# Pairing the heads of the gated linear attention, and loading constants later, in a hybrid encoder kernel

## The reference

```
def gla_chunk(S, inp):                       # one chunk of 64 frames, state S [64 x 128] per head
    q, k, v, la = inp
    b = cumsum(la, axis=2)                   # log decay
    decay = exp(where(causal, b[t] - b[s], -inf))            # per key channel
    scores = einsum('bhtd,bhsd,bhtsd->bhts', q, k, decay)
    o = einsum('bhts,bhsv->bhtv', scores, v) + einsum('bhtd,bhdv->bhtv', q * exp(b), S)
    S_new = exp(b_end)[..., None] * S + einsum('bhsd,bhsv->bhdv', k * exp(b_end - b), v)
    return S_new, o
```

## Time and profile before

| | |
|---|---|
| runs | 3391.13, 3376.59, 3386.97 us, median 3386.97 |
| profiled execution | 3374.3 us, span 3372.3 us, mean granted TensorE clock 0.977 |
| PE busy | 3237.7 us, 96% of the span |
| PE weight loads busy | 2759.2 us, 82% |
| DVE, ACT, POOL busy | 56%, 49%, 28% |
| DMA | 356.61 MB, mean 106 GB/s |

### The profile page before, as it was taken

The page is one execution under the profiler, slowest core; times in us unless marked ns, Lnnn a source line. Parts: engine busy times, 40 slices in busy tenths (PEclk is TensorE's granted clock), DMA queues, the critical chain, the costliest instruction groups (busy, mean ns, idle before and its releaser), DMA issues. The chain is left out here.

```text
span 3372.3 us, 48730 instructions
## 1 busy us (share of the span) xinstructions
PE 3237.7 (96%) x18362; PEld 2759.2 (82%) x18362; DVE 1882.9 (56%) x3387; ACT 1663.6 (49%) x3129; POOL 929.4 (28%) x570
## 2 busy tenths in 40 slices
PE   6999999999977999999999999999999999999999
PEld 5777777787767888888988888898878887899998
DVE  2463544544436555554676766677778776323333
ACT  3443343523327555554566665567666665233332
POOL 0231321411311233333323232322222223333332
PEclk9999999999886999999999999999999999999999
DMA  4553443533336223332523233242222223422221
GB/s 138 154 173 105 143 143 105 176 99 105 99 102 175 79 82 103 94 107 80 174 76 95 85 99 105 88 150 68 84 76 88 93 71 101 135 67 84 76 87 66
DMA packets 272378, 356.61 MB, mean 106 GB/s; under 512 B 59713, under 2 KB 188754, under 8 KB 271122
## 3 DMA queue, kind: packets, MB, share of 16 engines
q1 hardware_dynamic: 272146, 353.50, 33.4%
HBM read 295.91 MB, written 57.54 MB: 105 GB/s over the span
## 5 line engine op out<-in xcount | busy, mean ns | idle before, releaser
L1825 POOL TENSOR_TENSOR st_ul<-st_ur,st_uh 128x1024 fp32r<-128x1024 f32 x144 | 343.3, 2406 | 845.1 <-ACT st_uh L1634 845.1
L1832 POOL TENSOR_TENSOR st_dl<-st_dr,st_dh 128x1024 fp32r<-128x1024 f32 x144 | 342.0, 2397 | 775.5 <-ACT st_dh L1644 775.5
L1799 DVE TENSOR_TENSOR st_ya<-st_ya,st_dp 128x512 f32<-128x512 f32 x544 | 369.1, 682 | 132.1 <-PE st_dp L1556 129.7
L1727 DVE TENSOR_TENSOR_SCAN st_g<-st_z,st_g,st_a 128x127 f32<-128x127 f32 (+3 forms) x336 | 371.3, 1105 | 19.9 <-DVE st_g L1716 0.5
L1786 DVE TENSOR_TENSOR st_tl<-st_dp,st_th 128x512 fp32r<-128x512 f32 (+3 forms) x166 | 96.6, 582 | 464.6 <-ACT st_dp L1682 464.5
L1601 ACT ACTIVATE st_a<-st_z 128x128 f32<-128x128 f32 (+3 forms) x336 | 177.1, 527 | 356.0 <-PE st_z L1415 214.8
L491 PE MATMUL fr_pj<-fr_wl,fr_xh 128*128 128x512 f32 x816 | 335.6, 411 | 0.0
L1556 PE MATMUL st_dp<-st_dh,st_tl 128*128 128x512 f32 x1020 | 335.2, 400 | 0.0
L1556 PE MATMUL st_dp<-st_dl,st_th 128*128 128x512 f32 x1020 | 334.9, 400 | 0.0
L1556 PE MATMUL st_dp<-st_dh,st_th 128*128 128x512 f32 x1020 | 334.3, 400 | 0.0
L1438 PEld LDWEIGHTS st_po<-st_v,st_wt 128*128 128x128 f32 x2256 | 310.7, 199 | 28.6 <-DMA st_v<-out_new_v 3.2
(11 more groups left out here) (169 smaller groups left out, 6063.9 us busy)
## 6 DMA issues: line engine op xcount, KB each, us to landing
st_ur<-in_w_up SPq DMA_DIRECT2D x60, 1024.0 KB, 5.3
st_dr<-in_w_down SPq DMA_DIRECT2D x60, 1024.0 KB, 4.9
fr_wr<-in_w_in SPq DMA_DIRECT2D x96, 512.0 KB, 3.9
k_t<-fr_stT SPq DMA_DIRECT2D x21, 512.0 KB, 4.4
fr_xb<-in_x SPq DMA_DIRECT2D x17, 512.0 KB, 5.5
q_t<-fr_stT SPq DMA_DIRECT2D x17, 512.0 KB, 4.6
st_ya<-in_x SPq DMA_DIRECT2D x17, 512.0 KB, 5.7
st_qh<-q_t SPq DMA_DIRECT2D x64, 128.0 KB, 6.2
```

Of the source, the lines that this page charges most:

```text
L1727: ins = dve.tensor_tensor_scan(g[:, u % 2, n - 2::-1], z[:, u % 2, n - 1:0:-1], a[:, u % 2, n - 2::-1], g[:, u % 2, n - 1:n], ALU.add, ALU ...
L1799: dve.tensor_tensor(part, part, dp[:, k % BANKS], ALU.add).then_inc(s_fd, 1)
L1825: pool.tensor_tensor(ul[:, c], ur[:, c], raw(uh[:, c]), ALU.subtract).then_inc(s_ul, 1)
L1832: pool.tensor_tensor(dl[:, k], dr[:, k], raw(dh[:, k]), ALU.subtract).then_inc(s_dl, 1)
```

## The change

In the linear attention the two heads of a pair are issued alternately. `sc0` and `sc1` (and `sc2`, `sc3`) are taken together: both banks are waited for, then the 7 multiplications of the head in partitions 0 to 63 and those of the head in 64 to 127 alternate, each head to its own bank. The output has two banks, `po0` for even and `po1` for odd heads; for each pair `sm` x `v` of both heads is followed by four multiplications of 64 rows and 64 columns, one for each head and chunk, each writing only the 64 rows of its chunk. The zero halves of `qb` and the semaphore `s_oe` go; ACT copies two half banks where it copied one bank. Planned times in the tile are shifted to suit.

The constants are split over three semaphores and loaded later: gains and `w_a2`, `b_a2` behind the first splits, GLA constants at planned time 2000, the broadcast of `norm2_g` in the second phase behind the loads of the first two heads. The first four weight splits and their rests are planned at -36e3, and so stand before the norms. `rests` on DVE follow the same `split` times. The two first weight slices are issued right behind `lt`.

```
-        order = (("pt", 0.0, "A"), ("pd00", 0.04, "A"), ("pd01", 0.08, "A"), ("pd10", 0.14, "A"), ("pd11", 0.18, "A"),
-                 ("sc0", 0.38, "D"), ("sc1", 0.42, "D"), ("pu0", 0.46, "D"), ("pu1", 0.49, "D"), ("sc2", 0.62, "D"), ("sc3", 0.66, "D"), ("po", 0.92, "A"))
+        order = (("pt", 0.0, "A"), ("pd00", 0.06, "A"), ("pd01", 0.06, "A"), ("pd10", 0.16, "A"), ("pd11", 0.16, "A"),
+                 ("sc0", 0.38, "D"), ("sc1", 0.38, "D"), ("pu0", 0.50, "D"), ("pu1", 0.50, "D"),
+                 ("sc2", 0.66, "D"), ("sc3", 0.66, "D"), ("po0", 0.92, "A"), ("po1", 0.92, "A"))
@@ split
-            return -20e3 + 100 * i
+            return -36e3 + 100 * i
@@ constants (SP)
                 yield -89e3
-                sp.dma_start(g64[:, 0], bcast_rows(qg, HD)).then_inc(s_c, 16)
-                sp.dma_start(g64[:, 1], bcast_rows(kg, HD)).then_inc(s_c, 16)
                 sp.wait_ge(s_cs, 2)
                 sp.dma_start(lt[:, 0, 0:KC * RANK]..., w_in[:, C_ALR:C_ALR + RANK]...).then_inc(s_wa, 16)
-                sp.dma_start(wa2[0:RANK, :], w_a2).then_inc(s_c, 16)
-                sp.dma_start(wa2[RANK:RANK + 1, :], b_a2).then_inc(s_c, 16)
-                yield -79e3
+                yield -35e3
+                (w_a2, b_a2, qg, kg).then_inc(s_cg, 16)
+                yield 2000.0
                 (sum_mats, end_mat, score_mask, 4 x gla_g).then_inc(s_cl, 16)
@@ w_loads
-                    yield -80e3 + k if k < 2 else plan.split(k - 2) + 200
+                    yield -88.5e3 + k if k < 2 else plan.split(k - 2) + 200
@@ gla (PE)
+                    if name in ("sc0", "sc2", "po0"):
+                        continue
-                    elif name[:2] == "sc":
-                        for i in range(NL):
-                            pe.matmul(bank[:, i * CHUNK:(i + 1) * CHUNK], kx[half, i, :], right(qx[half, i, :], i), start=True, stop=True)
-                        mm = pe.matmul(bank[:, NL * CHUNK:SCOLS], qkT[half, 2 + a, :], qkT[half, a, :], start=True, stop=True)
+                    elif name in ("sc1", "sc3"):
+                        banks = [gp[:, plan.gp.bank(f"sc{2 * a + e}", t)] for e in range(2)]
+                        for i in range(NL):
+                            for e, half in enumerate(halves):
+                                pe.matmul(banks[e][:, i * CHUNK:(i + 1) * CHUNK], kx[half, i, :], right(qx[half, i, :], i), start=True, stop=True)
+                        for e, half in enumerate(halves):
+                            pe.matmul(banks[e][:, NL * CHUNK:SCOLS], qkT[half, 2 + a, :], qkT[half, a, :], start=True, stop=True).then_inc(s_gp, 1)
-                        for e in range(2):
-                            if e:
-                                pe.wait_ge(s_oe, t + 1)
-                            for a in range(2):
-                                pe.matmul(dst, sm[:, hd, NL * CHUNK:SCOLS], v[:, p, hd * DV:(hd + 1) * DV], start=True, stop=False)
-                                pe.matmul(dst, qb[half, p, a, 0:P], st[half, p, 0, a], start=False, stop=False)
-                                mm = pe.matmul(dst, qb[half, p, a, P:2 * P], st[half, p, 1, a], start=False, stop=True)
+                        banks = [gp[:, plan.gp.bank(f"po{e}", t)] for e in range(2)]
+                        for a in range(2):
+                            for e in range(2):
+                                pe.matmul(banks[e][:, a * DV:(a + 1) * DV], sm[:, hd, NL * CHUNK:SCOLS], v[:, p, hd * DV:(hd + 1) * DV],
+                                          start=True, stop=False)
+                            for c, tok in enumerate(halves):
+                                for e, half in enumerate(halves):
+                                    mm = pe.matmul(banks[e][tok, a * DV:(a + 1) * DV], qb[half, p, a, tok], st[half, p, c, a],
+                                                   start=False, stop=True)
@@ constants (ACT: am, ae)                                @@ constants (POOL: gain of q)
-                yield -9e3                                         -   yield -68e3
-                act.wait_ge(s_c, 16 * (2 + 4 + 3 + GLA_HEADS))     -   pool.wait_ge(s_c, 16 * (2 + 4 + 3 + GLA_HEADS))
+                yield 9000.0                                       +   yield 3000.0
+                act.wait_ge(s_cl, 16 * (3 + GLA_HEADS))            +   pool.wait_ge(s_cg, 64)
@@ gla_rows (ACT)
-                    act.activation(on[:], gp[:, plan.gp.bank("po", t)], ACT.Copy).then_inc(s_gpa, 1)
+                    for e in range(2):
+                        act.activation(on[...][:, :, e], gp[:, plan.gp.bank(f"po{e}", t), 0:2 * DV]..., ACT.Copy).then_inc(s_gpa, 1)
@@ DVE
-            dve.memset(qb[:], 0.0).then_inc(s_sp, 1)
-    masked at 0.43, 0.47, 0.68, 0.71; new_states at 0.50, 0.51; products at 0.23, 0.52; level_sums at 0.58, 0.75
+    masked at 0.42, 0.44, 0.70, 0.72; new_states at 0.52, 0.54; products at 0.20, 0.55; level_sums at 0.60, 0.76
@@ phase_stream (SP; PE, ACT, DVE wait for s_c at 32)
-            sp.dma_start(gb[:], bcast_rows(norm_g, D)).then_inc(s_c, 16)
             load_kq(0), load_v(0), load_kq(1), load_v(1)
+            sp.dma_start(gb[:], bcast_rows(norm_g, D)).then_inc(s_gb, 16)
```

More of the change, by code:

```diff
@@ L428, in gla_loads @@
                     if t >= 2:
-                        sp.wait_ge(s_gp, plan.gp.full("po", t - 2))
+                        sp.wait_ge(s_gp, plan.gp.full("po1", t - 2))
                     sp.dma_start(v[:, p], rows(gv, t)).then_inc(s_v[p], 16)
@@ L523, in pieces @@
                         pe.wait_ge(s_ttd, plan.tt.freed("alr", b, 0, 1))
+                        if b == 0 and j == 0:
+                            pe.wait_ge(s_cg, 64)
                         mm = pe.matmul(bank[:, 0:256], alrT[0:RANK + 1, j * P:(j + 1) * P], wa2[0:RANK + 1, :], start=True, stop=True)
@@ L551, in gla @@
                             mm = pe.matmul(bank[:, hi - lo:512], ae[:], lal[:, a * P:(a + 1) * P], start=False, stop=True)
-                    elif name[:2] == "sc":
-                        hd = int(name[2])
-                        a, half = hd // 2, halves[hd % 2]
+                    elif name in ("sc1", "sc3"):
+                        a = int(name[2]) // 2
+                        banks = [gp[:, plan.gp.bank(f"sc{2 * a + e}", t)] for e in range(2)]
                         pe.wait_ge(s_kx, 2 * t + a + 1)
@@ L743, in gla_rows @@
                         act.wait_ge(s_md, 16 * t)
-                    act.wait_ge(s_gp, plan.gp.full("po", t))
-                    act.activation(on[:], gp[:, plan.gp.bank("po", t)], ACT.Copy).then_inc(s_gpa, 1)
+                    for e in range(2):
+                        act.wait_ge(s_gp, plan.gp.full(f"po{e}", t))
+                        act.activation(on[:].rearrange("p (a e d) -> p a e d", e=2, d=DV)[:, :, e],
+                                       gp[:, plan.gp.bank(f"po{e}", t), 0:2 * DV].rearrange("p (a d) -> p a d", d=DV), ACT.Copy).then_inc(s_gpa, 1)
                     yield plan.gla(t, 0.95)
-                    act.wait_ge(s_gpa, plan.gp.freed("po", t))
+                    act.wait_ge(s_gpa, plan.gp.freed("po1", t))
                     if t:
@@ L870, in products @@
                     if t >= 2:
-                        dve.wait_ge(s_gp, plan.gp.full("po", t - 2))
-                    dve.tensor_tensor(qb[:, t % 2, a].rearrange("p (c x) -> p c x", x=3 * CHUNK)[:, :, 0:CHUNK],
-                                      ex[:, a, NL * P:DCOLS].rearrange("p (c x) -> p c x", x=CHUNK),
-                                      qkT[:, a].rearrange("p (c x) -> p c x", x=CHUNK), ALU.mult).then_inc(s_qb, 1)
+                        dve.wait_ge(s_gp, plan.gp.full("po1", t - 2))
+                    dve.tensor_tensor(qb[:, t % 2, a], ex[:, a, NL * P:DCOLS], qkT[:, a], ALU.mult).then_inc(s_qb, 1)
             def end_keys():
@@ L884, in masked @@
                 for t in range(TILES):
-                    for hd, x in enumerate((0.43, 0.47, 0.68, 0.71)):
+                    for hd, x in enumerate((0.42, 0.44, 0.70, 0.72)):
                         yield plan.gla(t, x)
@@ L888, in masked @@
                             dve.wait_ge(s_am, 2)
-                            dve.wait_ge(s_c, 16 * (2 + 4 + 3 + GLA_HEADS))
+                            dve.wait_ge(s_cl, 16 * (3 + GLA_HEADS))
                         if t:
-                            dve.wait_ge(s_gp, plan.gp.full("po", t - 1))
+                            dve.wait_ge(s_gp, plan.gp.full("po1", t - 1))
                         dve.wait_ge(s_gp, plan.gp.full(f"sc{hd}", t))
@@ L898, in new_states @@
                     for c in range(2):
-                        yield plan.gla(t, 0.50 + 0.01 * c)
+                        yield plan.gla(t, 0.52 + 0.02 * c)
                         dve.wait_ge(s_gp, plan.gp.full(f"pu{c}", t))
@@ L1387, in next_v @@
                         load_v(k)
-            for k in range(2):
-                load_kq(k)
-                load_v(k)
+            load_kq(0)
+            load_v(0)
```

(5 more changed lines are left out.)

48 lines of the change are left out of this document (28 added, 20 removed).

## The result

The changed kernel takes 3245.43 us in the median (3242.54 to 3250.07, 4 runs) against 3382.28 (4 runs) for the kernel before, run beside it. The ratio is 0.959 [0.957, 0.962]: 137 us less, where 108 were forecast. The median lies 10 us under the low end of the range. The direction was right, and so were the two largest terms; two others had been put at nothing.

The account below looks back on a forecast made before the run. TensorE, busy 96% of the span, was taken to bound the kernel. Terms 64.6 + 36 + 5.5 + 3 + 1 - 2 = 108 us off a median of 3387 gave 3279, stated as 3278; range 3255 to 3340.

Parts of the forecast that it names:

- scores, 34 pairs: Attention scores in the first phase: alternating halves of rows overlap fully, each pair saves 1.90 us, 64.6 us in all.
- outputs, 17 tiles: Attention output of each tile: quarters of the array all overlap, saving 2.12 us a tile, 36 us in all.
- the two state updates side by side: State updates in the first phase: both planned at 0.50, priced only for the mask wait, no saving of their own.
- granted clock in phase 1: TensorE's clock in the first phase: no gain in the sum; fewer falls around 870 only in the range's low end.
- waits: the mask's gone, new ones: PE's first-phase waits: 5.5 us before the state update vanish; new ones cost 2 us, between 0 and 10.
- start: Before and just behind the first dense multiplication: dense work 0.9 us earlier, later waits gone, 3 us together.
- hand-over: Between the phases: without the broadcast ahead in the queue, first queries land 0.5 to 2 us earlier; 1 taken.
- second phase: GLA work after the hand-over: the forecast sum contains no term for it.
- given back: Rival, last five tiles: new PE waits return part of the gain, 30 us, giving 3308; chance 0.10.
- The step from the profiled execution to the median: From profiled 3266 to the median: the old kernel's 12.7 us offset kept, 3387 - 108 = 3279, stated as 3278.
- no overlap: Rival, attention scores: halves of rows do not run side by side; 50 us saved in all, 3337; chance 0.24.
- Slower through the clock: Rival, first phase: packed pieces lower the granted clock, one fall per pair costs 170 us, giving 3448; chance 0.03.

## Why the prediction came out too small

Step by step, for the profiled pair, in us (prices of pieces from their timelines, the clock from the lengths of its falls):

| step | forecast | measured |
|---|---|---|
| scores, 34 pairs | 64.6 | 66 |
| outputs, 17 tiles | 36 | 39.3 |
| the two state updates side by side | 0 | 12.8 |
| granted clock in phase 1 | 0 | 12.8 |
| waits: the mask's gone, new ones | 5.5 - 2 | -7.4, what is left of phase 1 |
| start | 3 | 3.3 |
| hand-over | 1 | 3.6 |
| second phase | 0 | -0.5 |
| sum | 108 | 129.9 (the pair: 129.8) |

Two terms failed that the prediction had put at nothing, the state updates and the clock: together 25.6 us, more than the 21.8 by which the sum was short.

- *Scores and outputs* were right in mechanism and size. The choice between full overlap and none, the one that carried most of the number, went the right way. Halves of rows overlap with their weight loads, as halves of columns did in the earlier trace rows.
- *State updates*: missed. The text on the mask step used their new planned time of 0.50 for the wait, but not for the cost: before, dense work stood between the two, each adding 0.79 us (344.69 to 345.94, less 0.46). Side by side they cost 0.81 and not 1.58; in two tiles the saving is 0.6. Where transpositions stand beside them, it is about 0.76 against the run with them apart. That makes 0.77 x 15 + 0.61 x 2 = 12.8. One change of shape there and back is saved, 0.39 by the 0.195 that the prediction had worked out for the output and didn't apply here; the rest is that the two chunks use different halves of the rows and run side by side, the same overlap that it had priced for the scores.
- *Clock*: the sum held it as it was and put the end of the falls only at the edge of the range. The prediction had seen the row, 0.75 between 860 and 880, without pricing the whole stretch. 35.8 us at the lower level became 10.2. The experiments tie it to the attention part; why it happens stays open.
- *Waits*: the mask wait was to go wholly; 1.9 us stayed. The new ones were bounded at 0 to 10 and taken at 2. There are 6.1 for `qx`, which the rival *given back* named, plus 1.9 still at the mask, 2.7 for the stacked operand and 1.2 in two single waits. That sum, 11.9, against the 8.2 of before (5.5, 2.0 for `qx` and 0.7 of smaller ones), is a loss of 4 where a gain of 3.5 was forecast. Phase 1 as a whole leaves a loss of 7.4; the other 3 or so are not listed as waits.
- *Start*: forecast 31.3 for the first dense multiplication, 31.17 measured; 23.3 for the first norm, 22.98 measured. That is 1.0, and the waits of 2.2 us behind it went as forecast.
- *Hand-over*: from the issue of the identity's load to the first product were 10.0 us and are 6.4. The issue saved is 0.4; the other 3.2 are the broadcast of one row of 4 KB to 128 partitions, which held up what stood behind it in the queue: the last of the loads that the product waits for took 6.3 us from issue to landing before and takes 3.1. The 0.5 to 2 us allowed for it were too little.
- *The step from the profiled execution to the median*: the 12.7 us between them were carried over from the kernel before. The changed kernel's profiled run lies 1 us under its median. An offset of one run is chance, not a property of the kernels; it makes up the other 12 of the 33 us between 3278 and 3245.43. It had no part in the 137 against 108 but for the 7 us between the pair and the medians.

Of the rivals, *no overlap* fell by the 24 passes in 1.39 us. *Given back* happened in a small part, the new waits. *Slower through the clock* had its sign wrong: with the packed pieces the granted clock was higher. The end of the first phase, put near 885, came at 862.

The Trainium skill's "TensorEngine Tiling (Array Packing)", Key Properties, with its rule that different tiles execute LdWeights and Matmul in parallel, is borne out, for 28 passes in the 1.96 us of a pair. The run with heads in turn adds to it that the passes must also be near each other in PE's order: 2.89 us with the same tiles.

## What to carry to other kernels

Where PE is the bound, look in its timeline for narrow passes that all use one half of the array, alternate them with those of the other half, and put narrow pieces next to each other: in the scores the first bought 66 us here, in the state updates the second took 13 off PE's work (5.7 of the time of phase 1, by the run with them apart). Naming different tiles isn't enough, the order counts too: with the heads in turn half of the scores' saving was gone. And when a change shifts planned times, price each piece whose neighbours change, not only the waits.

## What the runs showed of the hardware that was not expected

- Two halves of rows with 128-column loads overlap fully, 0.058 us a pass. Quarters run four at a time: 8 passes in 0.38 us, against 0.65 with twice the columns; 16 passes of two chunks in 0.61 us, where 8 of one chunk took 0.59.
- PE reaches ahead for a free half only partly: 2.89 us a pair in turn, 1.96 alternating. The 13th pass started before the 10th to 12th, so passes for different halves don't start strictly in order.
- The granted clock over the last five tiles was 0.88 with half-array pieces in them, but 0.96 and 0.97 with both halves busy, even with more such passes. With alternating heads every fall stood beside a wait of PE, with heads one after the other nine did not.
- A broadcast of one row to 128 partitions, 512 KB, delayed the loads behind it by about 3.2 us; in the pair of kernels with one half of the change each, the first product came 2.9 us later with it.
- Two traces of the changed kernel have a phase 1 equal to 0.2 us, while their second phases differ by 5.4 us. So a change in one stage is best read from that stage.
